# Block-diagonal weights for both heads and 32x32 turns on VectorE in the inverse of a delta-rule kernel

## The reference, cut to what matters

```python
def step(S, inp):
    r_t, w_t, k_t, v_t, kk_t, kka_t = inp
    sa = jnp.einsum('bhvk,bhk->bhv', S, kk_t)
    S = (S * w_t[:, :, None, :]
         - sa[..., None] * kka_t[:, :, None, :]
         + v_t[..., None] * k_t[:, :, None, :])
    y_t = jnp.einsum('bhvk,bhk->bhv', S, r_t)
    return S, y_t
```

## Time and profile before

| what | value |
|---|---|
| three runs | 2127.84, 2128.80, 2129.37 us, median 2128.8 |
| profiled execution: span from the first to the last instruction | 2125.2 us |
| granted TensorE clock, mean | 0.990 of full speed |
| TensorE matmul busy | 2028.3 us, 95% of the span, x16558 |
| TensorE weight load busy | 1629.9 us, 77% |
| VectorE busy | 1421.8 us, 67%, x2272 |
| ScalarE busy | 1004.1 us, 47% |
| GpSimd busy | 174.2 us, 8% |
| recurrence of eight turns and the finishing one | about 430 to 850 us of the span |

### The profile page before, as it was taken

One profiled execution on the slowest core, in us unless ns is written; L12 is line 12 of the kernel. 1 busy time (PEld: TensorE's weight loads), 2 busy tenths in 40 slices (PEclk: granted clock), 3 DMA queues, 4 the chain that ended last, 5 costly groups with the idle time before them and its releaser, 6 DMA issues.

```text
span 2125.2 us, 42655 instructions
## 1 busy us (share of the span) xinstructions
PE 2028.3 (95%) x16558; PEld 1629.9 (77%) x16558; DVE 1421.8 (67%) x2272; ACT 1004.1 (47%) x1765; POOL 174.2 (8%) x183
## 2 busy tenths in 40 slices
PE   6999999988988889999999999999999999999998
PEld 4877777777777776888888888888667778887876
DVE  7788888876666664555653656699777776445355
ACT  6666666645666655342331323442665434233233
POOL 5230000001333222200000000000000000000000
PEclk9999999999999999999999999999999999999999
DMA  4445555653333322233333333333113323333332
GB/s 123 119 143 174 163 172 177 187 127 74 93 77 92 86 60 72 80 94 103 90 99 90 99 99 89 99 89 99 40 50 101 98 60 89 99 89 92 96 88 80
DMA packets 395952, 215.19 MB, mean 101 GB/s; under 512 B 85136, under 2 KB 374312, under 8 KB 395816
## 3 DMA queue, kind: packets, MB, share of 16 engines
q1 hardware_dynamic: 395608, 213.18, 35.0%
q10 hardware_dynamic: 208, 0.06, 0.0%
HBM read 181.68 MB, written 31.52 MB: 100 GB/s over the span
## 4 chain that ended last, share of the span: by engine, by line
PE 86%; DVE 7%; ACT 3%; issue 3%; DMA 1%; SPq 1%; POOL 0%; DVEq 0%; ACTq 0%; POOLq 0%
PE bank L1912 24%; PE bank L1914 23%; PE bank L1913 23%; PE bank L596 3%; PE bank L573 1%; PE bank L604 1%; PE bank L506 1%; PE bank L520 1%; PE bank L547 1%; PE bank L1108 1%; PE bank L526 1%; ACT inv L821 1%; PE bank L539 1%; DVE inv L922 1%; PE bank L553 1%
## 5 line engine op out<-in xcount | busy, mean ns | idle before, releaser
L1912 PE MATMUL bank<-xl,w_hi 128*128 128x512 f32 x1568 | 619.1, 395 | 7.7 <-DVE xl L2634 2.7
L1914 PE MATMUL bank<-xl,w_hi 128*128 128x512 f32 x1568 | 610.9, 390 | 0.0
L1913 PE MATMUL bank<-xl,w_lo 128*128 128x512 f32 x1568 | 610.6, 389 | 0.0
L1558 ACT ACTIVATE w_hi<-w_raw 128x1024 fp32r<-128x1024 f32 x278 | 292.4, 1052 | 357.6 <-PE bank L1914 353.2
L2203 DVE TENSOR_TENSOR w_lo<-w_raw,w_hi 128x1024 fp32r<-128x1024 f32 x278 | 342.7, 1233 | 106.5 <-ACT w_hi L1558 99.8
L1912 PEld LDWEIGHTS bank<-xl,w_hi 128*128 128x128 f32 x1568 | 294.3, 188 | 95.1 <-issue 25.4
L1914 PEld LDWEIGHTS bank<-xl,w_hi 128*128 128x128 f32 x1568 | 294.3, 188 | 62.0
L1913 PEld LDWEIGHTS bank<-xl,w_lo 128*128 128x128 f32 x1568 | 294.5, 188 | 59.3 <-issue 0.5
L1912 PE MATMUL bank<-xh,w_hi 128*128 128x512 f32 x448 | 183.6, 410 | 11.0 <-DVE xh L2208 10.7
L1914 PE MATMUL bank<-xh,w_hi 128*128 128x512 f32 x448 | 176.0, 393 | 0.0
L1913 PE MATMUL bank<-xh,w_lo 128*128 128x512 f32 x448 | 175.9, 393 | 0.0
(11 more groups left out here) (385 smaller groups left out, 3173.5 us busy)
## 6 DMA issues: line engine op xcount, KB each, us to landing
w_raw<-in_a_w_in SPq DMA_DIRECT2D x64, 512.0 KB, 4.2
w_raw<-in_b_w_in SPq DMA_DIRECT2D x64, 512.0 KB, 4.1
w_raw<-in_w_ffn_up SPq DMA_DIRECT2D x42, 512.0 KB, 4.0
w_raw<-in_w_in SPq DMA_DIRECT2D x36, 512.0 KB, 3.8
w_raw<-in_a_w_out SPq DMA_DIRECT2D x16, 512.0 KB, 4.1
w_raw<-in_b_w_out SPq DMA_DIRECT2D x16, 512.0 KB, 3.9
w_raw<-in_w_ffn_down SPq DMA_DIRECT2D x16, 512.0 KB, 4.1
d_g<-sq SPq DMA_DIRECT2D x16, 256.0 KB, 2.3
```

The costliest lines, as they stand in the source:

```text
L1558: A(w_hi[0:rows, slot, 0:nkb, 0:ncol], w_raw[0:rows, slot, 0:nkb, 0:ncol], ACT.Copy).then_inc(s_hi, units)
L1912: mm(outp, wh, xlo, start=start, stop=False)
L1913: mm(outp, wl, xhi, start=False, stop=False)
L1914: return mm(outp, wh, xhi, start=False, stop=stop)
```

## The change

The block diagonals: `nix16` becomes `nixd`, a 128x128 float16 matrix per chunk with the two heads' 64x64 matrices on its diagonal and zeros in the corners, and `nixlo16` becomes `nixlod` in the same way. The corners are zeroed once on GpSimd ahead of the recurrence. `newton_v`, `residual` and `diagonal` then issue one matmul for both heads (`both_heads`), 128x128 weights, in place of two. VectorE writes the diagonal in two operations of 64 partitions instead of one of 128 (L918), and likewise the masked start (L922); GpSimd writes the low part in two halves, one after the other (L1046).

The turns: step 9 is gone, and everything of levels 1 to 5, residual and last inverse moves up one step, so that three steps with the chain alone are left at the end of a turn. The first inverse is now the 32x32 blocks of the start, each turned by VectorE (`turned_blocks`, after the memset of step 8). In levels 1 to 4 `newton_x` makes only one of its two products; ScalarE copies all four groups, 256 columns each, and VectorE no longer copies the fourth. The other form is made by VectorE in the next level's step, right behind each group's `w16`: a turn of 32x32 blocks from `inv2[:, 0]` to `inv2[:, 1]`, for which `newton_x` waits (`x_turned`). Level 5 makes and copies both as before. `rhs` only moves to another place.

```diff
@@ -246,6 +246,7 @@
+        nixd = [over("nixd0", [P, NCH, P], F16)]
@@ -257,10 +258,11 @@
-        nix16 = [over(f"nix16_{a}", [P, NCH, C], F16) for a in range(2)]
+        rhs = over("rhs", [P, 2, C])
+        nixd.append(over("nixd1", [P, NCH, P], F16))
@@ -274,10 +276,10 @@
-        nixlo16, w16 = ([over(f"{n}_{a}", [P, NCH, C], F16) for a in range(2)] for n in ("nixlo16", "w16"))
-        rhs = over("rhs", [P, 2, C])
+        nixlod = [over(f"nixlod{a}", [P, NCH, P], F16) for a in range(2)]
+        w16 = [over(f"w16_{a}", [P, NCH, C], F16) for a in range(2)]
@@ -480,7 +482,7 @@
-        S_FIRST, S_LEVELS, S_RESIDUAL, S_LAST = 9, 10, 20, 21
+        S_LEVELS, S_RESIDUAL, S_LAST = 9, 19, 20
@@ -600,48 +602,55 @@
-                for hs in rows:
-                    mm(bank[n][hs, 0:4 * C], (two16 if twice else one16)[hs, hs], eyes4[hs], start=True, stop=False,
-                       skip_group_check=True)
-
-            def first_inverse(t):
-                pe.wait_ge(R["turned_copied"], TURNED[3] * (t + 1))
-                pe.wait_ge(R["products_masked"], 4 * (t + 1))
-                for n, (a, g) in enumerate(GROUPS):
-                    pe.wait_ge(R["q0_made"], 4 * t + n + 1)
-                    each(n, 0, inv2[a][:, 1], eyes16).then_inc(R["r0_summed"], 1)
+                mm(bank[n][:, 0:4 * C], (two16 if twice else one16)[:], eyes4, start=True, stop=False,
+                   skip_group_check=True)
+
+            def both_heads(n, lhsT, rhs_, stop=True):
+
+                g = GROUPS[n][1]
+                for c in range(4):
+                    last = mm(bank[n][:, c * C:(c + 1) * C], lhsT[:, 4 * g + c, :], rhs_[:, 4 * g + c, :], start=False,
+                              stop=stop, skip_group_check=True)
+                return last
...
                 if level == 0:
-                    pe.wait_ge(R["r0_copied"], 4 * t + n + 1)
-                elif n < 3:
-                    pe.wait_ge(R["x_copied"], 15 * t + 3 * (level - 1) + n + 1)
+                    pe.wait_ge(R["x0_made"], 4 * t + n + 1)
+                elif level < 5 or n < 3:
+                    pe.wait_ge(R["x_copied"], 19 * t + 4 * (level - 1) + n + 1)
                 else:
-                    pe.wait_ge(R["x3_copied"], 5 * t + level)
+                    pe.wait_ge(R["x3_copied"], t + 1)
...
+                if level == 1:
+                    pe.wait_ge(R["turned_copied"], TURNED[3] * (t + 1))
+                    pe.wait_ge(R["products_masked"], 4 * (t + 1))
                 for n, (a, g) in enumerate(GROUPS):
...
                     diagonal(n, True)
-                    each(n, 0, nix16[a], inv2[a][:, 0], start=False).then_inc(R["v_summed"], 1)
+                    both_heads(n, nixd[a], inv2[a][:, 0]).then_inc(R["v_summed"], 1)
...
                     pe.wait_ge(R["v_copied"], 20 * t + 4 * (level - 1) + n + 1)
-                    each(n, 0, inv2[a][:, 1], w16[a])
-                    each(n, 4 * C, w16[a], inv2[a][:, 1]).then_inc(R["x_summed"], 1)
+                    if level > 1:
+                        pe.wait_ge(R["x_turned"], 16 * t + 4 * (level - 2) + n + 1)
+                    last = each(n, 0, inv2[a][:, 1], w16[a])
+                    if level == 5:
+                        last = each(n, 4 * C, w16[a], inv2[a][:, 1])
+                    last.then_inc(R["x_summed"], 1)
...
                 for n, (a, g) in enumerate(GROUPS):
-                    pe.wait_ge(R["low_made"], 2 * t + a + 1)
+                    pe.wait_ge(R["low_made"], 4 * t + 2 * a + 2)
                     inverse_ready(t, 5, n)
                     diagonal(n, False)
-                    each(n, 0, nixlo16[a], inv2[a][:, 0], start=False, stop=False)
-                    each(n, 0, nix16[a], inv2[a][:, 0], start=False).then_inc(R["e_summed"], 1)
+                    both_heads(n, nixlod[a], inv2[a][:, 0], stop=False)
+                    both_heads(n, nixd[a], inv2[a][:, 0]).then_inc(R["e_summed"], 1)
@@ -705,8 +714,6 @@
                                 fill(4)
-                        elif s == S_FIRST:
-                            first_inverse(t)
                         elif S_LEVELS <= s < S_LEVELS + 10:
@@ -855,15 +862,13 @@
                                 R["state_zeroed"][1], 1)
-                        elif s == S_FIRST:
-                            for n, (a, g) in enumerate(GROUPS):
-                                act.wait_ge(R["r0_summed"], 4 * t + n + 1)
-                                copy(inv2[a][:, 0, 4 * g:4 * g + 4, :], heads(n)).then_inc(R["r0_copied"], 1)
                         elif S_LEVELS <= s < S_LEVELS + 10 and (s - S_LEVELS) % 2:
                             level = (s - S_LEVELS) // 2 + 1
-                            for n in range(3):
+                            for n in range(4 if level < 5 else 3):
+                                a, g = GROUPS[n]
                                 act.wait_ge(R["x_summed"], 20 * t + 4 * (level - 1) + n + 1)
-                                inverse_copy(copy, n).then_inc(R["x_copied"], 1)
+                                (copy(inv2[a][:, 0, 4 * g:4 * g + 4, :], heads(n)) if level < 5 else
+                                 inverse_copy(copy, n)).then_inc(R["x_copied"], 1)
                         elif s == S_RESIDUAL:
@@ -890,6 +895,7 @@
             incl, strict = masks[:, 0:C], masks[:, P:P + C]
             dve.wait_ge(s_const, 3)
@@ -915,12 +921,17 @@
                 dve.wait_ge(R["nix_made"], 8 * t + 2 * n + 2)
-                TT(nix16[a][:, cr, :], nix[a][:, cr, :], eyes[:, cr, :], ALU.subtract).then_inc(R["nix16_made"], 1)
+                if t == 0 and n < 2:
+                    dve.wait_ge(R["corners_zeroed"], n + 1)
+                for hs in halves:
+                    TT(nixd[a][hs, cr, hs], nix[a][hs, cr, :], eyes[hs, cr, :], ALU.subtract).then_inc(
+                        R["nix16_made"], 1)
                 TT(st_q[t % 2][C:P, a, cr, 0, :], p0[C:P, :, 0, :], wide(strict, C, P, 4), ALU.mult)
                 TT(st_q[t % 2][0:C, a, cr, 2, :], p1[0:C, :, 1, :], wide(strict, 0, C, 4), ALU.mult)
-                dve.wait_ge(R["nix16_made"], 4 * t + n + 1)
-                TT(inv2[a][:, 1, cr, :], nix16[a][:, cr, :], bmask[:, 0, :].unsqueeze(1).to_broadcast([P, 4, C]),
-                   ALU.mult).then_inc(R["q0_made"], 1)
+                for h, hs in enumerate(halves):
+                    dve.wait_ge(R["nix16_made"], 8 * t + 2 * n + h + 1)
+                    TT(inv2[a][hs, 1, cr, :], nixd[a][hs, cr, hs], bmask[hs, 0, :].unsqueeze(1).to_broadcast([C, 4, C]),
+                       ALU.mult).then_inc(R["q0_made"], 1)
@@ -928,6 +939,12 @@
                     R["products_masked"], 1)
+
+            def turned_blocks(n, to, signal):
+
+                a, g = GROUPS[n]
+                V.transpose(inv2[a][:, to, 4 * g:4 * g + 4, :].rearrange("p c k -> p (c k)"),
+                            inv2[a][:, 1 - to, 4 * g:4 * g + 4, :].rearrange("p c k -> p (c k)")).then_inc(R[signal], 1)
@@ -973,6 +990,9 @@
                         V.memset(sv[b][0:C, :, 0, 0, :], 0.0).then_inc(R["state_zeroed"][0], 1)
+                        for n in range(4):
+                            dve.wait_ge(R["q0_made"], 8 * t + 2 * n + 2)
+                            turned_blocks(n, 0, "x0_made")
                     elif S_LEVELS <= s < S_LEVELS + 10 and (s - S_LEVELS) % 2 == 0:
@@ -982,10 +1002,13 @@
                              if level < 5 else V.tensor_copy(dst, heads(n))).then_inc(R["v_copied"], 1)
+                            if level > 1:
+                                dve.wait_ge(R["x_copied"], 19 * t + 4 * (level - 2) + n + 1)
+                                turned_blocks(n, 1, "x_turned")
                     elif S_LEVELS <= s < S_LEVELS + 10:
-                        level = (s - S_LEVELS) // 2 + 1
-                        dve.wait_ge(R["x_summed"], 20 * t + 4 * level)
-                        inverse_copy(V.tensor_copy, 3).then_inc(R["x3_copied"], 1)
+                        if (s - S_LEVELS) // 2 == 4:
+                            dve.wait_ge(R["x_summed"], 20 * t + 20)
+                            inverse_copy(V.tensor_copy, 3).then_inc(R["x3_copied"], 1)
                     elif s == S_RESIDUAL:
@@ -1041,9 +1064,12 @@
-                gp.wait_ge(R["nix16_made"], 4 * t + 3 + a)
+                gp.wait_ge(R["nix16_made"], 8 * t + 6 + 2 * a)
                 o(G.tensor_tensor(nix[a][:], nix[a][:], eyes[:], ALU.subtract))
-                G.tensor_tensor(nixlo16[a][:], nix[a][:], nix16[a][:], ALU.subtract).then_inc(R["low_made"], 1)
+                for h, hs in enumerate((slice(0, C), slice(C, P))):
+                    G.tensor_tensor(nixlod[a][hs, :, hs], nix[a][hs], nixd[a][hs, :, hs], ALU.subtract).then_inc(
+                        R["low_made"], 1)
+                    gp.wait_ge(R["low_made"], 4 * t + 2 * a + h + 1)
@@ -1537,7 +1563,12 @@
+            gp.wait_ge(s_unit, U_MIX + 3 * (CI - 1) + 2)
+            for m in nixd:
```

(8 more changed lines are left out.)

4 lines of the change are left out of this document (2 added, 2 removed).

## The result

The changed kernel takes 2151.7 us (median of 4 runs, 2149.8 to 2154.4); the kernel before, beside it on the same chip, 2128.7. The ratio is 1.0112, with a 95% interval of 1.0097 to 1.0126. So it is slower, by 23 us where 32 were forecast. The profiled span grew from 2125.2 to 2148.1 us, +22.9, and that is what has to be explained. A run lies 1.7 us above its own span (the profiled one 2149.82 above 2148.1); the rest of the 3.6 us between median and profiled span is how far that run was from the median.

The account below looks back on a forecast made before the run. TensorE looked like the bound, with VectorE behind in steps 0 to 8. 4.5 + 0.2 - 0.9 + 0.7 = +4.5 us a turn, 27 for six, plus 2.5 each for turns 0 and 1: +32, 2161 us; range 2118 to 2196.

Parts of the forecast that it names:

- Steps 5 to 8, +4.5 us a turn: Halved VectorE operations, each half waiting for a GpSimd operation, end this part 4.5 us later in turns 2 to 7.
- the rival in which the second half slips through: VectorE's second half starts straight behind the first, before GpSimd: 1.8 us a turn, 2143 us in all; chance 0.17.
- A transpose, 0.41 us: Price of one VectorE transpose, taken from L922, float16 from SBUF to SBUF with 256 columns.
- The faster rival: Transposes at half price, 0.28 us each, decided at 0.32; with halves getting through 2120 us, else 2138; chance 0.13.
- the slower one: Transposes at 0.69 us each: 5.6 us more a turn, 2206 us in all; chance 0.07.
- Levels 2 to 4, 4.3 us each: Length of a level: four `w16` 1.42, four transposes 1.42, evacuation 0.28 and wait 1.18 us.
- levels 1 to 4: -0.9: Levels 1 to 4 go from 16.7 to 15.8 us a turn, with the stops for instructions then hidden.
- +0.7: Level 5 to turn's end: transposes add 1.42 us, one more chain step 0.9; stops of 0.95 and some 0.65 go.
- The first inverse, from the last masked start to the first `w16`: Four VectorE transposes, 1.42 us, replace 32 matmuls and four ScalarE copies: +0.2 us a turn, between 0 and +0.4.
- Turns 0 and 1, 2.5 us each: With only `low_part` and no `finish` in the way, these turns lose 2.5 us each, between 1.8 and 4.5.
- The clock rival: TensorE, with fewer matmuls, is granted half speed in the levels: +4 us a turn, 2193 us; chance 0.07.
- No change: The fetch stops of TensorE cost more than seen and their loss pays for VectorE's work; chance 0.08.

Follow-up runs that it names:

- e3: The changed kernel with GpSimd's `finish` and `low_part` held back until VectorE has made all four masked starts of the turn; 2122.0 us, ratio 0.9997 to the kernel before.

## Why the prediction was right, and its size not

**Steps 5 to 8, +4.5 us a turn: right, by its own mechanism.** Measured +4.5; third group 16.6 us after the start of the turn, fourth 23.6, both within 0.1 of the working. e3 shows that it is GpSimd. The rule that each half waits for a GpSimd operation of its own is what happened in seven of eight halves, and the rival in which the second half slips through is out. The one exception costs nothing: the first `nixd` half of the third group, which the forecast had waiting as well, ran through. The Trainium skill (SBUF — State Buffer, Who interferes with whom) has the two-input operations of VectorE and GpSimd's block each other for a whole instruction; the trace agrees (0.86 us a pair alone, 2.01 and 2.17 beside GpSimd). The 18 transposes, with one input, that ran wholly inside a GpSimd operation took 0.38 to 0.40 us, no longer than the others.

**A transpose, 0.41 us: right** (0.420 mean of 160). The faster rival needed 0.32, the slower one 0.69; both are out. In level 2 the two forms alternate with starts 0.31 and 0.35 us apart. The figure of the Trainium skill (VectorE: DVE Perf Modes, The three transpose paths) made an estimate of 0.44, 0.02 too high.

**Levels 2 to 4, 4.3 us each: right** (4.07, 4.56, 4.24). Level 1 was to take 2.9 and takes 3.34; it is 2.91 in e3, where TensorE stands still for 1.4 us ahead of it in place of 3.58.

**The step that failed is "levels 1 to 4: -0.9", with the "+0.7" behind it.** Steps 9 to 23 were to come out even and lost 1.6 us a turn, nearly all of the distance between 32 and 23. Both old lengths were read from one turn, 16.7 and 11.1 us; the means of turns 1 to 7 are 18.1 and 9.1, because the stops fall at other places of each turn. So I split each length, for turns 1 to 7, into its stops and the rest.

Levels 1 to 4: the turn that I read has 1.7 us of stops in them, the mean is 2.8. Without the stops they were 15.3 us and are 16.2, +0.9; the forecast had 15.0 (16.7 less 1.7) becoming 15.8, +0.8. So the work was right and the stops were too small: -1.9 in place of -0.9.

Level 5 to the end: the turn that I read has 3.1 us of stops there, the forecast took away 1.6, and the mean is 1.1. Without the stops it was 8.0 us and is 9.25, +1.2, where the forecast had 1.42 for the transposes and 0.9 for the further step, 2.3 together. So here the work was too large, and the sum is +0.2 in place of +0.7. Which of the two terms was too large is open.

The first inverse, from the last masked start to the first `w16`, took 2.64 us and takes 2.69: +0.05 in place of +0.2. The mechanism of the stops was in the prediction; their mean over the turns, one view away, was not.

**Turns 0 and 1, 2.5 us each:** +4.1 and +0.4, 0.5 less in sum than forecast. The estimate lay between the halves alone and halves that are held; `low_part` by itself holds them nearly as long: in turn 1 steps 5 to 8 grow by 4.05 us (7.85 to 11.90), which steps 9 to 23 give back in large part (30.44 to 27.44), since the stops go there too.

**The clock rival** happened in small: the clock does fall, behind TensorE's idle time ahead of step 9, and costs 0.4 us a turn (level 1 against e3), not 4.

**"No change", because the loss of the stops pays for VectorE's work,** had the right mechanism and too small a prize. All the stops together are 28 us; the halves beside GpSimd alone cost 27 (4.5 x 6), and the transposes come on top.

## What to carry to other kernels

Before an edit that moves work from a busy engine to another, sum the waits of the busy one by what released them, over all repetitions and not one: two edits that cure the same wait are together worth little more than one of them. A whole operation that is split in two on an engine that another one can hold pays the other one's operation twice, so keep it whole or move the other engine's work to where the first one reads PSUM. What stands in an in-order queue behind work that it does not need, here the `w16` behind a transpose, is worth an attempt at another order before the work itself is given up.
